# A 32x32-blockwise VectorE transpose in four levels of a triangular inverse, in place of TensorE transposes and a ScalarE copy

## The reference, cut to what matters

```python
a_mat = jnp.where(strict, beta[..., :, None] * kk * decay_mat, 0.0)
eye = jnp.eye(c, dtype=jnp.float32)
sol = lax.linalg.triangular_solve(eye + a_mat, rhs, left_side=True, lower=True,
                                  unit_diagonal=True)
```

```python
proj = jnp.einsum("btd,dc->btc", h, w_in[l])
...
merged = jax.nn.sigmoid(g_gdn) * y_gdn + jax.nn.sigmoid(g_moba) * y_moba
x = x + jnp.einsum("btd,de->bte", merged, w_o[l])
```

## Time and profile before

| what | value |
|---|---|
| time, median of 3 runs | 1585.48 us (1585.01 to 1586.07) |
| span of the profiled execution, first to last instruction | 1583.4 us |
| busy: PE / DVE / ACT / POOL | 98% / 68% / 50% / 12% of the span |
| busy PEld (weight loads) | 82% of the span |
| granted TensorE clock | 1.000 of full speed |

### The profile page before, as it was taken

The page is one execution under the profiler, slowest core; times in us unless marked ns, Lnnn a source line. Parts: engine busy times, 40 slices in busy tenths (PEclk is TensorE's granted clock), DMA queues, the critical chain, the costliest instruction groups (busy, mean ns, idle before and its releaser), DMA issues.

```text
span 1583.4 us, 20787 instructions
## 1 busy us (share of the span) xinstructions
PE 1559.0 (98%) x7767; PEld 1299.2 (82%) x7767; DVE 1084.3 (68%) x1331; ACT 797.1 (50%) x1063; POOL 191.0 (12%) x181
## 2 busy tenths in 40 slices
PE   6999999999999999999999999999999999999999
PEld 6888888888888888888888888888888887887787
DVE  6655655745646646656558778867676999978864
ACT  5434534444445445445445347556565765555542
POOL 4202001002002001011011011010101111102020
PEclk9999999999999999999999999999999999999999
DMA  8314315224234224233234338667557777878783
GB/s 270 90 32 126 81 34 149 56 62 123 54 86 115 70 57 121 60 81 98 60 86 118 119 135 252 209 171 254 131 188 191 234 234 238 231 225 176 224 183 57
DMA packets 198048, 217.04 MB, mean 137 GB/s; under 512 B 7843, under 2 KB 140198, under 8 KB 196902
## 3 DMA queue, kind: packets, MB, share of 16 engines
q1 hardware_dynamic: 177030, 162.73, 34.0%
q0 software_dynamic: 20960, 53.52, 14.7%
HBM read 191.03 MB, written 29.39 MB: 139 GB/s over the span
## 4 chain that ended last, share of the span: by engine, by line
PE 92%; DVE 3%; issue 2%; ACT 1%; DMA 1%; SPq 0%; DVEq 0%; ACTq 0%
PE bank L823 15%; PE bank L827 15%; PE bank L825 14%; PE bank L1273 11%; PE bank L1275 11%; PE bank L1277 11%; PE bank L852 2%; PE bank L928 2%; PE bank L946 1%; DVE ring_lo L2282 1%; PE bank L1023 1%; PE bank L931 1%; PE bank L857 1%; PE bank L873 1%; PE bank L874 1%
## 5 line engine op out<-in xcount | busy, mean ns | idle before, releaser
L823 PE MATMUL bank<-h_hi_r,w_hi 128*128 128x512 f32 x1008 | 408.2, 405 | 0.0
L827 PE MATMUL bank<-h_hi_r,w_raw_r 128*128 128x512 f32 x1008 | 395.0, 392 | 0.0
L825 PE MATMUL bank<-h_lo_r,w_hi 128*128 128x512 f32 x1008 | 393.4, 390 | 0.0
L2282 DVE TENSOR_TENSOR ring_lo<-operands,ring_hi 128x1024 fp32r<-128x1024 f32 x224 | 271.5, 1221 | 112.6 <-ACT ring_hi L1646 111.9
L1646 ACT ACTIVATE ring_hi<-operands 128x1024 fp32r<-128x1024 f32 x224 | 235.4, 1060 | 214.2 <-PE bank L1277 161.9
L827 PEld LDWEIGHTS bank<-h_hi_r,w_raw_r 128*128 128x128 f32 x1008 | 189.1, 188 | 41.8
L823 PEld LDWEIGHTS bank<-h_hi_r,w_hi 128*128 128x128 f32 x1008 | 189.7, 188 | 35.6
L825 PEld LDWEIGHTS bank<-h_lo_r,w_hi 128*128 128x128 f32 x1008 | 189.9, 188 | 34.7
L1273 PE MATMUL bank<-ring_hi,h_hi_r 128*128 128x512 f32 x480 | 190.2, 396 | 1.3 <-issue 1.3
L1275 PE MATMUL bank<-ring_lo,h_hi_r 128*128 128x512 f32 x480 | 188.6, 393 | 0.0
L1803 DVE TENSOR_TENSOR w_raw_r<-w_raw,w_hi 128x2048 fp32r<-128x2048 f32 x64 | 151.4, 2365 | 37.2 <-ACT w_hi L1333 36.0
(11 more groups left out here) (333 smaller groups left out, 2183.1 us busy)
## 6 DMA issues: line engine op xcount, KB each, us to landing
w_raw<-in_w_in_dram SPq DMA_DIRECT2D x64, 1024.0 KB, 6.0
operands<-in_w_in_dram SPq DMA_DIRECT2D x64, 512.0 KB, 4.6
operands<-in_w_o_dram SPq DMA_DIRECT2D x32, 512.0 KB, 5.2
operands<-in_w_in_dram POOLq DMA_DIRECT2D x16, 512.0 KB, 8.2
gates<-e_block POOLq DMA_DIRECT2D x16, 512.0 KB, 5.7
operands<-in_w_out_gdn_dram SPq DMA_DIRECT2D x16, 512.0 KB, 5.0
operands<-gates SPq DMA_DIRECT2D x16, 512.0 KB, 7.0
operands<-in_w_out_moba_dram SPq DMA_DIRECT2D x16, 512.0 KB, 5.4
```

The lines of the kernel that those rows point to most:

```text
L823: pe.matmul(PJ[slot % 2][:], w_hi[slot % 2][:, c], h_hi[:, k, :], start=(k == 0), stop=False, skip_group_check=True)
L825: pe.matmul(PJ[slot % 2][:], w_hi[slot % 2][:, c], h_lo[:, k, :], start=False, stop=False, skip_group_check=True)
L827: mm = pe.matmul(PJ[slot % 2][:], w_lo[slot][:, c], h_hi[:, k, :], start=False, stop=(k == KT - 1), skip_group_check=True)
L2282: dve.tensor_tensor(ring_lo[:, n % RINGS, :], operand(q, p, j), ring_hi[:, n % RINGS, :].bitcast(F32), ALU.subtract).then_inc(s["op_lo"], 1)
```

## The change

At the levels 4 to 32 (k = 0 to 3) the transposes of line 931 and the ScalarE copy of line 1417 are gone. In their place VectorE transposes `xa` straight into `XTt` with one instruction, `turned(h, k)`. It transposes each 32x32 block in its place; since at these levels all that is not zero in `xa` lies in diagonal blocks of at most 32, this is the whole transpose. `turned` stands on VectorE behind `qk` at level 4, and directly behind the `mb` step of the level before at the others. With it the wait for qkd in `ma(h, 0)` is gone, as the bank G1 is no longer written there. The level 64 is as it was.

```diff
@@ TensorE, ma
                 if k == 0:
                     pe.wait_ge(s["X2"], h + 1)
-                    pe.wait_ge(s["qkd"], h + 1)
...
                     for t in range(NT):
-                        pe.matmul(G0[:m, t * PAIRED:(t + 1) * PAIRED], Ln[:, t * P:t * P + m],
-                                  half_tile(xa, t, b, 1), start=True, stop=True)
-                    for t in range(NT):
-                        mm = pe.transpose(G1[:m, t * P:t * P + m], xa[:m, t * P:t * P + m], ident[:m, :m])
+                        mm = pe.matmul(G0[:m, t * PAIRED:(t + 1) * PAIRED], Ln[:, t * P:t * P + m],
+                                       half_tile(xa, t, b, 1), start=True, stop=True)
                 mm.then_inc(s["ma_mm"], 1)
@@ ScalarE, ma and its calls
-            def ma(h, k):
-
-                act.wait_ge(s["ma_mm"], NL * h + k + 1)
-                if k == NL - 1:
-                    act.activation(corner(Yt, 1), corner(G0, 1), ACT.Copy).then_inc(s["Y"], 1)
-                else:
-                    m = P - LEVELS[k]
-                    act.activation(q4(XTt)[:m, :, :m], q4(G1)[:m, :, :m], ACT.Copy).then_inc(s["XT"], 1)
+            def ma(h):
+
+                act.wait_ge(s["ma_mm"], NL * h + NL)
+                act.activation(corner(Yt, 1), corner(G0, 1), ACT.Copy).then_inc(s["Y"], 1)
...
-                ma(h, 2)
                 silu(h, 2)
-                ma(h, 3)
                 zsig(h, 0)
-                ma(h, 4)
+                ma(h)
@@ VectorE
+            def turned(h, k):
+
+                if k == 0:
+                    dve.wait_ge(s["X2"], h + 1)
+                else:
+                    dve.wait_ge(s["X"], NL * h + k)
+                dve.transpose(XTt[:], xa[:]).then_inc(s["XT"], 1)
+
...
                 n2(h)
                 qk(h)
+                turned(h, 0)
...
                 mb(h, 0)
+                turned(h, 1)
...
                 mb(h, 1)
+                turned(h, 2)
...
                 mb(h, 2)
+                turned(h, 3)
                 split(n + 5, 1)
                 ma(h, 3)
```

More of the change, by code:

```diff
@@ L1524, in head @@
                     softmax(p, 2)
-                ma(h, 0)
                 if p is not None:
@@ L1529, in head @@
                     pTc(p, 2)
-                ma(h, 1)
-                if p is not None:
                     pTc(p, 3)
```

## The result

In the same five rounds the changed kernel takes 1577.14 us (median; 1574.21 to 1579.69) and the kernel before 1585.96 us (1585.01 to 1586.44). The ratio is 0.9944, with a 95% interval of 0.9933 to 0.9954: 0.56% faster, 8.8 us. The forecast was 1574.2 us with a range of 1571.8 to 1578.0.

What follows compares the result with a forecast made beforehand. TensorE bounds the kernel; VectorE and ScalarE work is hidden. Savings 7 x 1.43 + 1.3 = 11.3 us, from 1585.5 to 1574.2 us, 0.7% faster; own range 1572.5 to 1576, whole range 1571.8 to 1578.0.

Steps and rivals of the forecast that it cites:

- rival A: VectorE's transpose is paid per 128x128 matrix, 1.24 us per instruction; TensorE waits at level 32; 1576.1 us; chance 0.09.
- Chain, and what bounds: TensorE holds 92% of the last-ending chain; a change is worth what it takes off TensorE, less new waits.
- What is taken off TensorE: Line 931's transposes at levels 4 to 32, start to start: 1.43 us a head, 11.4 us in eight heads.
- The pair 0.74 and 0.72: Level 16, head 3: transposes start 0.74 us after ma's product, a window 0.72 us after mb's, so TensorE is freed.
- Rival C: TensorE's transposes lie in the shadow of weight loads; with half the 11.4 us shadow, about 1580 us; chance 0.04.
- t: Cost of one new VectorE transpose from its start to the next start, taken as 0.61 us, bounds 0.42 and 1.67.
- D: Rival: VectorE takes float32 in four passes, 2.76 us per transpose; TensorE waits for masks; slower, 1595 us; chance 0.02.
- B: Rival: VectorE's transpose costs the upper bound, 1.67 us; head 3 waits 0.53 us; 1580.3 us; chance 0.07.
- Room at level 32: Head 3, mask's end on VectorE to TensorE's product: 0.58 us, no wait; head 7 at level 8: 0.23 us.
- Head 0: VectorE sets the time at level 32; saves 1.3 us if level 16's end waits only for TensorE's product, otherwise 0.65.
- Base of the sum: Span of before 1583.4 us; runs' median 2.1 us above it, taken as unchanged, giving 1585.5 us to subtract from.
- The second half moves as a whole: The program's second half starts when the heads are done, its transfers released by the same products; as long as before.

Runs made afterwards that it cites:

- e2_keep_pe: Changed kernel, but TensorE still makes its four transposes per level into a bank nobody reads, wait for qkd back: 1585.74 us, ratio 0.9997 to the kernel before.

## Why the prediction was right, point by point

The median, 1577.1 us, lies in the whole range (1571.8 to 1578.0) and outside the forecast's own (1572.5 to 1576). The mechanism in the heads held nearly to the number, 11.0 us against 11.3. That the median still fell into the whole range is in part luck: about 2.5 us were lost in the second half, which the sum had at nothing, and the range had been stretched past 1576 for rival A, whose cause is out.

- **Chain, and what bounds.** Right: e2_keep_pe shows that the rest of the change is worth nothing without TensorE's part.
- **What is taken off TensorE, 1.43 us a head by starts.** Measured 1.39. The sum by durations, 33.8 us, would have been three times too much. So would the estimate of 35 us from the 275 ns of the Trainium skill (TensorE: Matmul & The Clock Gate, Part 4: PE-mode transpose). The pair 0.74 and 0.72 read rightly; the window now follows after 0.71. Rival C is out.
- **t, taken as 0.61 us.** The instruction is 711 ns long, against the 0.69 us of the row that it was taken from. Its cost in the queue is 1.09 us from the end step of level 16 to the split (433.66 to 434.75), less the 0.33 us that this distance was: 0.76 us. Of the 0.15 us more, 0.12 come ahead of it: it starts 0.45 us behind the instruction whose result it reads, where the split, which reads nothing of it, started 0.33 us behind. Rivals A and D are out, B's price too. One argument against A was misread: that a row with 512 elements costs more only when it moves data between partitions. In the trace of before line 1957 (128x512, no such move) took 0.42 us in the median and 1.52 once, and line 1981, which does read one set of partitions and write another, took 0.69 us, while line 1982 took 1.67. What makes the slow ones slow isn't shown, and the slow rows say nothing for or against A. The trace agrees with the Trainium skill's Vector Engine (DVE) Microarchitecture Reference, section 3.8 (one element per cycle and lane): four matrices of 128 columns cost what 512 elements cost elsewhere, and the estimate of 1.24 us from four times 311 ns did not hold.
- **Room at level 32, 1.19 - t.** With 0.76 that is 0.43; measured 0.46. In head 7 at level 8 the formula 0.84 - t gives 0.08. The mask there ends at 873.48 and the product starts at 873.59, 0.11 us. The prediction was near its edge here: 0.1 us more on VectorE, and TensorE would have waited. These are the rows of head 7, the mask and then the product:

```profile
873.06 0.42 DVE L1905 TENSOR_TENSOR work<-bank,pairs 120x256 f32<-120x256 f32 x1
...
873.59 0.67 PE L943 MATMUL bank<-work 120*120 120x64 f32 x5
```
- **Head 0.** The product of level 32 starts at 100.67 instead of 102.28 us; 0.3 of these 1.6 us are there at the first level already, which leaves 1.3, as taken. Of the two cases of the prediction it is the one that it took: the end of level 16 no longer waits for the sigmoid but for TensorE's product, and VectorE still sets the time, as TensorE waits 0.24 us for the mask. VectorE's end of level 16 and TensorE's product of level 32:

```profile
96.94 0.42 DVE L1920 TENSOR_TENSOR inv_a<-bank,inv_a 112x256 f32<-112x256 f32 x1 [0.90 <-PE bank L943]
...
100.67 0.89 PE L943 MATMUL bank<-work 96*96 96x64 f32 x8 [0.24 <-DVE work L1905]
```
- **Base of the sum.** The profile of before has a span of 1583.4 us and the medians of before were 1585.5 and 1586.0. The time of a profiled execution of the changed kernel is 1.6 us above its span (1574.21 and 1572.6). By the same distance the profiled execution of before took 1585.0 us and was one of the shorter ones, so the 2.1 us of the prediction were half a microsecond too many.
- **The second half moves as a whole.** This step failed: the padding wins back 2.5 to 2.7 us of the median, and the profiled second halves of the unpadded changed kernel take 639.3 to 642.5 us instead of 638.8. It starts when the heads are done, and its issues do stand at the same times in it, but the fetches of TensorE's own instructions don't move with it. 96 instructions fewer shifted them by 6 us against the transfers, into GpSimd's store and loads. That the fetch delays the store, and that padding brings the time back, is shown; that this one fetch makes the whole loss is argued from the profiles, since the padding moves the others too. The prediction had named a part of the gain lost to "some other wait that I don't see", and put it into VectorE's queue in head 7. It wasn't there: from the first product of the inverse in head 7 to the second half it is 71.36 us before and 70.02 us after, 1.34 of 1.43 us gained.

## What to carry to other kernels

Price what leaves a pipelined TensorE by the distance of starts, not by durations, and check with a like pair of rows that the next instruction can take the place. A step put on an engine that is hidden costs what it pushes the first waited-for result beyond its room: write the room as a number, here 1.19 - t, find what stands in between, and the head with the least. When two kernels agree in every issue of a stretch and differ in its length, look at transfers that nobody in the program issued, such as the fetches of instructions. Here a few idle instructions at the start were worth 2.5 to 2.7 us beside a gain of 11.0.

## What the runs showed of the hardware

A blockwise VectorE transpose of 128x512 float32 takes 711 ns, 704 to 714 in 32 of them, as an elementwise instruction of the size does (0.69 us).

The profile lists fetches of instructions (queue 8) among the packets of the DMA engines that also move the data. In the second half a fetch of 16 KB is made every 29 us on average (23 to 34 us apart in the profile of the changed kernel), and its place follows the number of TensorE's instructions that stand in the program ahead of it, a loop's body counted once: 96 fewer moved it from 21 to 27 us, 48 padding transposes (96 instructions with their weight loads) moved it back to 20.9. Counted as executed the numbers don't fit: 256 fewer in eight heads would then have moved it no further than the 96 of the padding, which ran once, moved it back. Beside such a fetch a store of 256 KB landed after 3.7 to 4.5 us instead of 2.3 us in five profiles of five, and loads of 512 KB after 8.0 to 8.9 instead of 6.8 us (medians of three) in three of the five.
